# Weight tiles end to end in shared rings, and another order of turns, second position sums and compressed softmax in the mixing stage

## What the kernel computes

```python
def first_block(x, p, ...):
    h = h + 0.5 * swiglu(rmsnorm(h, norm_ffn1), ffn1_w1, ffn1_w3, ffn1_w2)       # "FFN a"
    z = rmsnorm(h, norm_mix) @ w_in
    q, kc, vc, ksl, vsl, kw, vw, g, u = jnp.split(z, split_at, axis=-1)
    q, kc, ksl, kw = rope(q), rope(kc), rope(ksl), rope(kw)
    o_nsa = nsa_attention(q, kc, vc, ksl, vsl, kw, vw, sigmoid(g), ...)
    o_s5 = s5_mixer(u, ...)                       # 32 groups, 64 states, complex scan over 512
    h = h + jnp.concatenate([o_nsa, o_s5], -1) @ w_out
    h = h + 0.5 * swiglu(rmsnorm(h, norm_ffn2), ffn2_w1, ffn2_w3, ffn2_w2)       # "FFN b"
    gate = sigmoid(rmsnorm(h, norm_ple) @ w_ple_gate)
    return rmsnorm(h + gate * (p @ w_ple), norm_final)

def compress(kv, pe, w1, w2):                     # windows of 32 positions, stride 16: 31 of them
    blk = kv[:, tok] + pe[None, None, :, None, :]          # "positions"
    return gelu(blk @ w1) @ w2                             # "squeeze", "hidden", "compressed"

# in nsa_attention, for each block of 128 queries
p_cmp = masked_softmax(einsum(qc, kc) * scale, c_end <= t)        # "weigh"
# top blocks are chosen by p_cmp; p_slc and p_win are two further masked softmaxes
o = g0 * p_cmp @ vc + g1 * p_slc @ v_sel + g2 * p_win @ v_w

def second_block(x, c, ...):
    for l in range(2):                            # "layer 0", "layer 1"
        mod = silu(c) @ w_ada[l] + b_ada[l]
        u = (rms_norm(x, norm_g[l]) * (1 + scale) + shift) @ w_in[l]
        rg_x, rg_z, ml_x, ml_o, ml_z = jnp.split(u, split_pts, axis=-1)
        y_rg = rglru(conv(rg_x), ...) * silu(rg_z)
        y_ml = mlstm_branch(ml_x, ml_o, ...) * silu(ml_z)
        x = x + gate * (jnp.concatenate([y_rg, y_ml], -1) @ w_out[l])
    return rms_norm(x, final_g)
```

## Time and profile before

| | |
|---|---|
| median of 3 runs | 2004.05 us (2002.74 to 2004.84) |
| the profiled execution | 2004.08 us, its span 2002.3 us, mean granted clock 0.981 |
| TensorE busy | 1928.0 us, 96% of the span |
| VectorE busy | 1186.0 us, 59% |
| ScalarE busy | 819.4 us, 41% |
| GpSimd busy | 337.5 us, 17% |
| transfers | 197.27 MB, 99 GB/s over the span |
| chain that ended last | TensorE 78%, VectorE 13%, ScalarE 4% |

### The profile page before, as it was taken

How to read it: one execution, slowest core, us unless ns; L and a number is a source line. 1 busy time by engine, 2 the same in 40 slices (tenths; PEclk the granted TensorE clock), 3 DMA queues, 4 the chain that set the end, 5 groups by cost and what they waited for, 6 DMA issues and landing times.

```text
span 2002.3 us, 22514 instructions
## 1 busy us (share of the span) xinstructions
PE 1928.0 (96%) x9010; PEld 1498.5 (75%) x9010; DVE 1186.0 (59%) x1519; ACT 819.4 (41%) x1211; POOL 337.5 (17%) x329
## 2 busy tenths in 40 slices
PE   6999999998998999999999899999999899999997
PEld 5788888775644788888888778776788778776786
DVE  5758344576764556656655787826753659346732
ACT  5232233311556343213334448545642466455531
POOL 2000000144420110001011212504201024115002
PEclk8999999998999999999999899999999899999998
DMA  5332223222002145645632222221222222221231
GB/s 196 102 107 84 95 95 116 78 75 96 27 1 69 64 151 186 220 147 186 208 111 84 74 92 85 94 93 35 74 95 95 95 82 74 93 76 32 95 97 61
DMA packets 53464, 197.27 MB, mean 99 GB/s; under 512 B 6000, under 2 KB 6512, under 8 KB 52848
## 3 DMA queue, kind: packets, MB, share of 16 engines
q1 hardware_dynamic: 43200, 160.55, 24.3%
q0 software_dynamic: 7648, 29.10, 4.4%
q10 hardware_dynamic: 2512, 6.18, 0.9%
HBM read 192.67 MB, written 2.10 MB: 97 GB/s over the span
## 4 chain that ended last, share of the span: by engine, by line
PE 78%; DVE 13%; ACT 4%; issue 2%; POOL 1%; DMA 1%; ACTq 0%; POOLq 0%; DVEq 0%
PE PS L599 77%; DVE AR L1666 3%; DVE WLO L1663 2%; DVE AR L2192 1%; ACT WHI L1196 1%; DVE AR L1696 1%; DVE TMP L2266 1%; DVE AR L2017 1%; PE PS L858 1%; DVE AR L2159 0%; DMA H<-in_xT 0%; ACT HX L1367 0%; POOL ACC L2324 0%; DVE H L2095 0%; ACT SQ L1211 0%
## 5 line engine op out<-in xcount | busy, mean ns | idle before, releaser
L599 PE MATMUL PS<-HNH,WHI 128*128 128x512 f32 x1632 | 656.7, 402 | 17.0 <-ACT HNH L1227 15.2
L1663 DVE TENSOR_TENSOR WLO<-RAW,WHI 128x1024 fp32r<-128x1024 f32 (+1 forms) x272 | 374.3, 1379 | 504.2 <-ACT WHI L1196 504.1
L599 PE MATMUL PS<-HNH,WLO 128*128 128x512 f32 x1632 | 639.2, 392 | 5.6 <-DVE WLO L1663 5.6
L1196 ACT ACTIVATE WHI<-RAW 128x1024 fp32r<-128x1024 f32 (+1 forms) x272 | 297.7, 1095 | 637.5 <-PE PS L599 579.2
L599 PE MATMUL PS<-HNL,WHI 128*128 128x512 f32 x1632 | 435.8, 390 | 0.1
L599 PEld LDWEIGHTS PS<-HNH,WHI 128*128 128x128 f32 x1632 | 307.9, 189 | 96.3 <-issue 21.6
L599 PEld LDWEIGHTS PS<-HNH,WLO 128*128 128x128 f32 x1632 | 308.0, 189 | 80.2 <-issue 9.1
L599 PEld LDWEIGHTS PS<-HNL,WHI 128*128 128x128 f32 x1632 | 307.3, 188 | 64.9 <-DVE HNL L1666 1.0
L2324 POOL TENSOR_TENSOR ACC<-ACC,SQ 128x512 f32<-128x512 f32 x46 | 62.4, 1357 | 802.8 <-ACT SQ L1211 801.8
L599 PE MATMUL PS<-AR 32*128 32x256 f32 (+14 forms) x852 | 162.9, 420 | 3.7 <-DVE AR L2057 1.5
L599 PE MATMUL PS<-HIDH,WLO 128*128 128x512 f32 x352 | 137.0, 389 | 0.0
(11 more groups left out here) (317 smaller groups left out, 2281.3 us busy)
## 6 DMA issues: line engine op xcount, KB each, us to landing
RAW<-in_w_in SPq DMA_DIRECT2D x80, 512.0 KB, 3.5
AR<-in_w_ada POOLq DMA_DIRECT2D x48, 512.0 KB, 3.9
RAW<-in_w13a SPq DMA_DIRECT2D x44, 512.0 KB, 3.4
RAW<-in_w13b SPq DMA_DIRECT2D x44, 512.0 KB, 4.1
RAW<-in_w_out SPq DMA_DIRECT2D x40, 512.0 KB, 3.5
RAW<-in_w2a SPq DMA_DIRECT2D x16, 704.0 KB, 4.1
RAW<-in_w2b SPq DMA_DIRECT2D x16, 704.0 KB, 4.9
RAW<-in_w_inA SPq DMA_DIRECT2D x12, 512.0 KB, 3.4
```

The lines of the kernel that those rows point to most:

```text
L599: return pe.matmul(o, l, r, start=start, stop=stop, skip_group_check=True)
L1196: act.activation(hi_of(name, i), raw_of(name, i), ACT.Copy).then_inc(*HI.up(name, i))
L1663: dve.tensor_tensor(lo_of(name, i), raw_of(name, i), f32(hi_of(name, i)), S_).then_inc(*LO.up(name, i))
```

## The change

There are two parts.

**Rings.** RAW, WHI and WLO keep their space, 4224 words a partition each. `shelve()` lays the tiles end to end in it and starts again at 0 where the next doesn't fit; it also gives, for each tile, the earlier ones that it overwrites. So four tiles of 1024 lie there at a time (or three of 1408, or more of 512). A transfer waits for the tiles that it overwrites and for the tile 6 before it, whose landing semaphore it uses; the half of a tile waits for all that it overwrites. `split_order()` follows these rules, so that splits stand at other turns than before. The halves are laid out over the split tiles alone.

**Order.** In `mix_order()` turn 6 follows turn 5 at qk 7 (before it stood after the first value tile), turn 7 stands after the first value tile (before after the second), positions 1 after the third (before ahead of the first). The compressed softmax, weigh 0 to 6, stands in rounds 0 to 6 (before in rounds 2 to 8).

```diff
+def shelve(sizes, space):
+    spots, at = [], 0
+    for k, n in enumerate(sizes):
+        at = 0 if at + n > space else at
+        spots.append((at, tuple(j for j in range(max(0, k - 12), k) if spots[j][0] < at + n and at < spots[j][0] + sizes[j])))
+        at += n
+    return spots
...
         if i > 5:
             yield "turn", i - 2
+        if i == 7:
+            yield "turn", 6
         if i >= 4:
             yield "squeeze", 0, i - 4
         yield from some(3)
-    yield "positions", 1
     for z in range(2):
         for tt in range(4):
             yield "v", z, tt
-            if z == 0 and tt < 2:
-                yield "turn", 6 + tt
+            if (z, tt) == (0, 0):
+                yield "turn", 7
+            if (z, tt) == (0, 2):
+                yield "positions", 1
...
-        if 1 < n < 9:
-            yield "weigh", n - 2
+        if n < 7:
+            yield "weigh", n
...
-        NSLOT, SLOT = 3, 1408
-        RAW = sb("RAW", NSLOT * SLOT)
+        NLAND, SHELF = 6, 3 * 1408
+        RAW = sb("RAW", SHELF)
...
-        NW = 3
-        WHI, WLO = sb("WHI", NW * SLOT, F32R), sb("WLO", NW * SLOT, F32R)
+        FIRST = 3
+        WHI, WLO = sb("WHI", SHELF, F32R), sb("WLO", SHELF, F32R)
...
+        raw_spot = shelve([n for _, _, n, _ in order], SHELF)
+        half_spot = shelve([place_of[s][2] for s in splits], SHELF)
+
         def split_order():
...
-                while nxt < len(splits) and place_of[splits[nxt]][0] < used + NSLOT and nxt < done + NW:
+                while nxt < len(splits):
+                    k = place_of[splits[nxt]][0]
+                    over = [k - NLAND, *raw_spot[k][1], *(place_of[splits[o]][0] for o in half_spot[nxt][1])]
+                    if max(over) >= used:
+                        break
                     ready.append(splits[nxt])
                     nxt += 1
                 yield ready
...
-                    if o >= NW:
-                        act.wait_ge(*P_.at(*splits[o - NW]))
+                    for over in half_spot[o][1]:
+                        act.wait_ge(*P_.at(*splits[over]))
...
-                if k >= NSLOT:
-                    before, j, _, was_split = order[k - NSLOT]
+                for over in sorted({*raw_spot[k][1], *range(max(k - NLAND, 0), k - NLAND + 1)}):
+                    before, j, _, was_split = order[over]
                     sp.wait_ge(*(LO if was_split else P_).at(before, j))
-                sp.dma_start(raw_of(name, i), D[name] if i is None else D[name][i]).then_inc(slot_sem[k % NSLOT], 16)
+                sp.dma_start(raw_of(name, i), D[name] if i is None else D[name][i]).then_inc(raw_sem[k % NLAND], 16)
```

More of the change, by code:

```diff
@@ L381, in program @@
         HI, LO = Sig(sem("s_weights_hi")), Sig(sem("s_weights_lo"))
-        slot_sem = [sem(f"s_raw_slot{i}") for i in range(NSLOT)]
+        raw_sem = [sem(f"s_raw_landed{i}") for i in range(NLAND)]
         ada_sem = [sem(f"s_ada_slot{i}") for i in range(2)]
@@ L404, in program @@
         splits = [(name, i) for name, i, n, split in order if split]
+        raw_spot = shelve([n for _, _, n, _ in order], SHELF)
+        half_spot = shelve([place_of[s][2] for s in splits], SHELF)
         def split_order():
-            done, nxt = 0, NW
-            for first in splits[:NW]:
+            nxt = FIRST
+            for first in splits[:FIRST]:
                 yield [first]
             for used in range(1, len(order) + 1):
-                done += order[used - 1][3]
                 ready = []
-                while nxt < len(splits) and place_of[splits[nxt]][0] < used + NSLOT and nxt < done + NW:
+                while nxt < len(splits):
[3 more added lines that the diff above has]
+                        break
                     ready.append(splits[nxt])
@@ L420, in raw_of @@
             k, o, n = place_of[name, i]
-            return RAW[:, k % NSLOT * SLOT:k % NSLOT * SLOT + n]
+            return RAW[:, raw_spot[k][0]:raw_spot[k][0] + n]
         def raw_in(name, i):
             k = place_of[name, i][0]
-            return slot_sem[k % NSLOT], 16 * (k // NSLOT + 1)
+            return raw_sem[k % NLAND], 16 * (k // NLAND + 1)
         def hi_of(name, i):
             k, o, n = place_of[name, i]
-            return WHI[:, o % NW * SLOT:o % NW * SLOT + n]
+            return WHI[:, half_spot[o][0]:half_spot[o][0] + n]
         def lo_of(name, i):
             k, o, n = place_of[name, i]
-            return WLO[:, o % NW * SLOT:o % NW * SLOT + n]
+            return WLO[:, half_spot[o][0]:half_spot[o][0] + n]
         def rows(v, b):
```

## The result

The changed kernel takes 1993.86 us (median of 4 runs, 1992.11 to 1995.58), the kernel before 2004.38 in the same runs: 10.5 us apart by the medians, at a ratio of 0.9942 (95% interval 0.9930 to 0.9955). In a later set of runs it was 0.9943 (0.9931 to 0.9956), 1992.72 us. The profiled execution took 1992.18 us, with a span of 1990.4; before it was 2004.08 and 2002.3. The forecast was 1993.0 and the range 1985 to 2000.

The account below looks back on a forecast made before the run. TensorE was taken to bound the kernel, busy 1928.0 of 2002.3 us. From 2004.08 us, -6.0 + 0.3 (PLE) - 1.65 - 9.2 + 5.5 + 0 = -11.05 gave 1993.0 us, range 1985 to 2000.

Parts of the forecast that it names:

- Part c: Turns 6, 7 and positions 1: bank wait of 7.2 us and slow clock go, new wait 1.0; -9.2 us.
- part b: Query tiles w_inA 10, 11, w_inV 0: earlier transfers take the wait off VectorE ahead of block 1's read; -1.65 us.
- Part d: Rounds 2 and 3: w_out splits right behind squeezes wait for transfers, stopping TensorE 2.4 and 3.1 us; +5.5 us.
- part e: Weighs two rounds earlier: 0.9 us won, 0.9 paid for a further half-speed spell; 0, bounds -5.0 and +4.
- Part a: FFN a, w_out stage and layers: deeper rings give splits one tile more lead, ending stops on WLO; -6.0 us.
- The spells: Half-speed clock stretches: the one at 1738.6 to 1745.4 us may come or go; 0, bounds -3.4 and +3.4.
- The signs: Profile signs: no stop above 2 us at 475-500 us, WLO waits about 1 us; wrong if new spells appear elsewhere.
- The contention of VectorE with GpSimd: Two w_out splits among GpSimd work cost up to 1.1 us more each, sum then 1995; left out.
- Rival 1: Blocks of w_out covered and the stops at 544.24 and 547.81 us go: 1984 us; chance 0.15.
- Rival 2: TensorE waits for GpSimd at the read of block 2 instead of the bank: 1998 us; chance 0.20 with Rival 3.
- Rival 3: VectorE late by its own queue, so the deeper ring's lead doesn't help: 1999 us; chance 0.20 with Rival 2.
- Rival 4: Slower: engines stand bare at splits of w_out 0, 1, 2 (18.6 us) plus two spells (7): 2013 us; chance 0.05.

Follow-up runs that it names:

- e2: The kernel before with the new order alone, its three ring slots kept: 1995.1 us, ratio 0.9959 to the kernel before.
- e6: The changed kernel with RAW back in three slots, WHI and WLO end to end: 1994.06 us, ratio 0.9947 to the kernel before.
- e8: The changed kernel with splits one turn behind the unsplit tile whose space they take, two behind a wv1 tile: 1979.74 us, ratio 0.9874.
- e3: The changed kernel with splits one turn behind the use of the unsplit tile whose space they take: 1983.75 us, ratio 0.9893.
- e4: The changed kernel with weigh 0 to 6 back in rounds 2 to 8: 1997.01 us, ratio 0.9958 to the kernel before.
- e5: The changed kernel with turns 6 and 7 and positions 1 back at their old places: 2001.34 us, ratio 0.9982.
- e7: The changed kernel with WHI and WLO back in three slots, raw tiles end to end: 1995.69 us, ratio 0.9953.

## Why the prediction was right, step by step

- **Part c, turns and positions (-9.2).** Right in kind and size. From the read of block 1 to the squeeze of round 2, 7.1 us are gained, and 2.2 of work moved in ahead: 9.3. The wait on GpSimd taken as 1.0 us was 0.30. e2 and e6 show that it is 2 to 2.6 us where part b is missing, which was the reason given for staying near the upper bound.
- **Part d, the blocks (+5.5), with part e (0).** Right in kind, place and releasers: a weigh's eviction and the gelu. The stops are 2.12 and 2.19 (2.4 and 3.1 were worked out), 0.53 less for the old one. The way of the first is the one worked out. That of the second isn't: its copy stood 1.04 us ahead of the table load but waited for no transfer, so the transfer of 3.5 us in its sum wasn't what held it, and that its size came near is luck. The slow clock behind them is 10.3 us long against 3.4 before, 3.5 us more lost, where I had 0.9; and the stop of 1.73 at the former 547.81 is gone. In all 10.8 gained fall to 6.35: +4.4 for d and e. Against e8, which has the same order of weighs and no blocks, the two blocks cost 5.8 us. The step that was wrong in itself is that the spell would be small.
- **Part a (-6.0)** came to 5.4 in sum, but not from the terms that it was added up from. The stop of 1.8 us at 83 us went, but VectorE was late elsewhere: 1.33 us at 182.46, for a half of a w2a tile behind a row of S5's preparations (L1715). FFN a gained 0.4 and not 1.8. The 0.8 of the w_out stage went, and 0.9 came up behind it at 701.90, where FFN b's first matmul waits for its activations: 0.1. The layers' four stops went and brought 4.9, not 3.4, since a stop costs more than its idle time. The matmuls overlap, and a stop breaks that up. Before:

```profile
1271.07 0.39 PE L599 MATMUL PS<-HNL,WHI 128*128 128x512 f32 x1
1271.30 0.39 PE L599 MATMUL PS<-HNH,WHI 128*128 128x512 f32 x1
1272.57 0.50 PE L599 MATMUL PS<-HNH,WLO 128*128 128x512 f32 x1 [0.88 <-DVE WLO L1663]
1272.90 0.39 PE L599 MATMUL PS<-HNH,WHI 128*128 128x512 f32 x1
```

  From start to start it is 0.23 us without a stop, 1.27 over the stop and 0.33 behind it, so the 0.88 us cost 1.14. Two such stops make 2.3 us in each layer; small steps bring the other 0.15. The premise that a stop is gone where the tile ahead of it is longer failed in FFN a and in the w_out stage: there the next late engine took most of it.
- **PLE (+0.3)** cost 0.2 up to 1119.21.
- **Part b (-1.65)** gave 1.0: the stop behind L2361 stayed, 0.76 us at 458.19, since GpSimd was the last there. VectorE's idle time ahead of the same three splits is 2.86 us in the changed kernel, all of it ahead of w_inA 11, in place of 14.3. The middle one of the three was 3.39 us before, and doesn't lie between 5.10 and 5.79 as the prediction says; the 14 us that it counts with are right:

```profile
460.42 1.53 DVE L1663 TENSOR_TENSOR WLO<-RAW,WHI 128x1024 fp32r<-128x1024 f32 x1 [3.39 <-ACT WHI L1196]
```

- **The spells.** Taken as nothing, they gave 3.4 us in layer 1 and took 1.7 in layer 0, in this execution. That is the luck in the number. The profiled execution gained 11.9 us against a forecast of 11.05; parts a and b were 1.25 short, d and e 1.1 better, the spells brought 1.7, and some 0.9 is lost in small steps that I can't place. By the runs' median the change is 10.5 us.
- **The signs.** Those of parts b and c showed: no stop above 0.30 us and full clock between 475 and 500 us, and at most 0.41 us of idle time ahead of the 1120-wide splits. Of the signs of being wrong one came true: a new spell away from all the places named, at 1302 us. Of those for part d ScalarE's idle time of 3 us ahead of a WHI didn't show, it was 1.31; the 3.11 us stood on VectorE. The waits for WLO sum to 1.7 us, not to about 1.
- **The contention of VectorE with GpSimd**, 2.2 us by the prediction's working, didn't show here. The two splits took 1.23 us each at 513.75 and 519.08; GpSimd had nothing running beside them. The Trainium skill's "SBUF — State Buffer", section "Who interferes with whom", says that a VectorE instruction with two SBUF inputs contends with a GpSimd instruction that reads SBUF. These two splits met none and so don't test it.
- **The rivals.** Rival 1 (1984) has the number of e3, 1983.75, but e3 still has one block; without any, in e8, the time is 1979.74, and the changed kernel has them all. Rival 2's wait is real where the rings are missing (e2), but 2.0 us long and not 7. Rival 3, where VectorE is late by its own queue and the lead doesn't help, fits the stop of 0.39 us in PLE alone, which stands in both kernels. Rival 4 was far off: two blocks cost 4.3 us of stops and 5.8 us in all, not 18.6 and two spells.

## What to carry to other kernels

A deeper ring lets work be issued earlier, and on an engine that goes through its program in order earlier is not always better. Where the space of a tile is released by the very step at which its copy is issued, the copy can stand in the queue for the length of a transfer (3.4 us here, from 509.30 to 512.66) and holds back all behind it; let it stand a step or two later than the release. That was one line here and brought another 14 us by the medians (0.68%), about half of it from a stop that was there before the change. Where a copy needs room in two rings, make both deeper: with either at three slots the splits of the layers stood where they had stood before. Count for each tile how many steps lie between the release of its space and its first reader in the program, and look at the places where this is none.

## What the runs showed of the hardware

- The same stop can be followed by half-speed clock or not. The wait at the first w_glu matmul, behind S5's gelu, is 2.37 us long in all kernels. In five of them (e2, e3, e4, e5, e7) a stretch at 0.50 follows it, of 3.4 or 6.8 us, in the others none does. The windows of e3 and then of e8:

```profile
602.90:606.30 3.40, 3.40 (x5) 1.35 (x4) 0.00 (x0) 3.39 (x12) 0.00 (x0) 0.50 0.00 0
```

```profile
598.96:605.00 6.04, 6.04 (x32) 3.05 (x34) 0.72 (x1) 6.01 (x15) 0.00 (x0) 1.00 0.00 0
```

- Half speed also comes without a stop, among small matmuls: 3.4 us at 1302 in the changed kernel with TensorE busy for the whole of it, and in layer 1 in the kernel before. One and the same kernel has two groups of times 3.5 us apart. That such spells make them isn't shown, since both profiled executions of the changed kernel (1992.18 and 1991.63) are of the faster group. An estimate for a change of some us must leave room for one or two spells, 1.7 us for each 3.4.
- A stop of TensorE among matmuls that overlap costs more than the idle time that the trace gives for it: 1.14 us for 0.88 at 1272.57 before the change.
